# Closing normalisation with five of sixteen tiles divided otherwise over VectorE, ScalarE and GpSimd

## The reference

```python
def layer_norm(x, g, b):
    xf = x.astype(jnp.float32)
    mu = jnp.mean(xf, -1, keepdims=True)
    var = jnp.mean(jnp.square(xf - mu), -1, keepdims=True)
    y = (xf - mu) * lax.rsqrt(var + LN_EPS) * g.astype(jnp.float32) + b.astype(jnp.float32)
    return y.astype(x.dtype)
...
        ff = hierarchical_moe(x, w_group[l], b_group[l], w_router[l], b_router[l], w_gate_up[l], w_down[l])
        x = layer_norm(ALPHA * x + ff, ln2_g[l], ln2_b[l])
```

## Time and profile before

| | us |
|---|---|
| median of 3 runs | 2767.09 (2764.66 to 2777.89) |
| profiled execution, its own time | 2769.08 |
| its span, first to last instruction | 2767.4 |
| busy TensorE / VectorE / ScalarE / GpSimd over the span | 2570.9 / 1623.0 / 1206.0 / 497.0 |
| last matmul of the experts ends | 2702.4 |
| first load of the closing normalisation is issued | 2711.24 |
| last wide VectorE operation ends | 2763.2 |
| end of the span | 2767.4 |

### The profile page before, as it was taken

One profiled execution on the slowest core, in us unless ns is written; L12 is line 12 of the kernel. 1 busy time (PEld: TensorE's weight loads), 2 busy tenths in 40 slices (PEclk: granted clock), 3 DMA queues, 4 the chain that ended last, 5 costly groups with the idle time before them and its releaser, 6 DMA issues. The chain is left out here.

```text
span 2767.4 us, 42797 instructions
## 1 busy us (share of the span) xinstructions
PE 2570.9 (93%) x13455; PEld 2178.0 (79%) x13456; DVE 1623.0 (59%) x3059; ACT 1206.0 (44%) x2066; POOL 497.0 (18%) x538
## 2 busy tenths in 40 slices
PE   6999998999999999979799999769999999999990
PEld 4888886788888888879688888558888888888880
DVE  6333232766666666649644444569575567557956
ACT  4111111445445454437311010358575577557956
POOL 1111111101101010025323333112111122112210
PEclk9999999899999999979899999879999999999995
DMA  6444536756565564369534443459798778779956
GB/s 213 134 152 132 165 126 190 216 187 198 185 192 182 189 205 162 119 145 237 180 114 136 136 133 133 154 205 369 247 315 304 243 265 304 255 233 329 368 186 250
DMA packets 261763, 566.40 MB, mean 205 GB/s; under 512 B 27056, under 2 KB 119984, under 8 KB 259616
## 3 DMA queue, kind: packets, MB, share of 16 engines
q1 hardware_dynamic: 172816, 432.34, 45.9%
q0 software_dynamic: 18720, 64.96, 9.2%
q10 hardware_dynamic: 70128, 67.84, 7.3%
HBM read 433.45 MB, written 131.60 MB: 204 GB/s over the span
## 5 line engine op out<-in xcount | busy, mean ns | idle before, releaser
L2417 DVE TENSOR_TENSOR e_wl<-rw_raw,e_wh 128x1024 fp32r<-128x1024 f32 (+1 forms) x384 | 446.8, 1219 | 26.1 <-ACT e_wh L2330 25.8
L2330 ACT ACTIVATE e_wh<-rw_raw 128x1024 fp32r<-128x1024 f32 (+1 forms) x384 | 376.9, 1049 | 6.4 <-PEq L76 6.4
L1190 PE MATMUL b_pg<-b_g_wh,jb_w_low 128*128 128x512 f32 x1024 | 336.6, 401 | 0.7 <-DVE b_g_out L1385 0.7
L2280 PE MATMUL e_p_gu<-e_wh,e_xh 128*128 128x512 f32 (+1 forms) x784 | 310.5, 396 | 1.5 <-DVE e_xl L2422 1.5
L2282 PE MATMUL e_p_gu<-e_wl,e_xh 128*128 128x512 f32 (+1 forms) x784 | 306.2, 391 | 0.0
L2281 PE MATMUL e_p_gu<-e_wh,e_xl 128*128 128x512 f32 (+1 forms) x784 | 305.6, 390 | 0.0
L1190 PEld LDWEIGHTS b_pg<-b_g_wh,jb_w_low 128*128 128x128 f32 x1024 | 184.7, 189 | 33.4 <-issue 1.1
L1247 ACT ACTIVATE b_th<-b_t 128x512 fp32r<-128x512 f32 (+3 forms) x160 | 85.4, 534 | 284.5 <-PE b_t L1172 275.7
L1190 PE MATMUL b_pg<-b_g_wl,jb_w_low 128*128 128x512 f32 x512 | 204.4, 399 | 0.0
L1329 DVE TENSOR_SCALAR_CACHE_REDUCE b_sc<-b_s 128x512 f32<-128x512 f32 (+3 forms) x320 | 179.4, 606 | 31.9 <-PE b_s L1159 18.6
L300 PE MATMUL j_pg<-qkv_w_hi,j_xh 128*128 128x512 f32 (+1 forms) x512 | 190.9, 373 | 6.7 <-DVE qkv_w_lo L475 6.7
(11 more groups left out here) (363 smaller groups left out, 5866.3 us busy)
## 6 DMA issues: line engine op xcount, KB each, us to landing
rw_raw<-w_gate_up SPq DMA_DIRECT2D x256, 512.0 KB, 7.8
rw_raw<-w_down SPq DMA_DIRECT2D x128, 512.0 KB, 9.4
jb_w_low<-xt_hi SPq DMA_DIRECT2D x64, 512.0 KB, 3.8
jb_w_low<-xt_lo SPq DMA_DIRECT2D x64, 512.0 KB, 4.9
gates<-b_g_out ACTq DMA_DIRECT2D x64, 256.0 KB, 5.2
m_gt<-gates SPq DMA_DIRECT2D x16, 1024.0 KB, 8.2
qk_hi<-j_staged ACTq DMA_DIRECT2D x15, 832.0 KB, 4.5
qk_lo<-j_staged ACTq DMA_DIRECT2D x15, 832.0 KB, 6.9
```

The lines of the kernel that those rows point to most:

```text
L1190: last = nc.tensor.matmul(pg[:], x_side, w_side, start=(q == 0), stop=(q == PASSES - 1))
L2280: nc.tensor.matmul(p_gu[p][:], xh[:, at], hi, start=(k == 0), stop=False)
L2330: nc.scalar.activation(wh[:, slot(e, s), :], raw[:, s:s + 1, :], ACT.Copy).then_inc(w_hi, 1)
L2417: nc.vector.tensor_tensor(wl[:, slot(e, s), :], raw[:, s:s + 1, :], f(wh[:, slot(e, s), :]), ALU.subtract).then_inc(w_lo, 1)
```

## The change

Five tiles, TURNS = 2, 4, 7, 9, 12, take another way; the eleven others (MAIN) keep theirs, and their waits count positions in MAIN. For a turned tile VectorE takes bn_stats of both halves and bn_aggr (`statistics`), ScalarE a root of the variance (`root_of_turn`), VectorE a reciprocal and a one-column product, minus mean times reciprocal (`ready`), ScalarE one pass row * rs + shiftby in place (`centre`), and GpSimd the multiplication by gamma and the addition of beta, both in place. `statistics(0)` stands behind average(0), the others behind shift of every second main tile but the last; `ready` stands between scale and shift. The tile's store waits for GpSimd (`polished`). The order of loads and stores on SP stays.

```diff
--- before.py
+++ after.py
@@ -2138,6 +2138,14 @@
         z, gam, bet, junk = raw[:, 0:ROWS, :], raw[:, ROWS, :], raw[:, ROWS + 1, :], py[:]
         total, off, square, sd, rs = (ph.sb(n, [P, NT]) for n in ("total", "off", "square", "sd", "rs"))
         eps = ph.sb("eps", [P, 1])
+
+        TURNS = (2, 4, 7, 9, 12)
+        MAIN = [t for t in range(NT) if t not in TURNS]
+        bn = ph.sb("bn", [P, len(TURNS), 2, 6])
+        mv = ph.sb("mv", [P, len(TURNS), 2])
+        shiftby = ph.sb("shiftby", [P, len(TURNS)])
+        bn_step, bn_done, bn_root, bn_inv, bn_ready, centred, bn_times, polished, bn_passed = (ph.sem(n) for n in (
+            "bn_step", "bn_done", "bn_root", "bn_inv", "bn_ready", "centred", "bn_times", "polished", "bn_passed"))
         complete, vec_in, eps_set, loaded = ph.sem("complete"), ph.sem("vec_in"), ph.sem("eps_set"), ph.sems("loaded", ROWS)
         summed, averaged, squared, sd_done, inverted, times, finished, warmed = (
             ph.sem(n) for n in ("summed", "averaged", "squared", "sd_done", "inverted", "times", "finished", "warmed"))
@@ -2178,7 +2186,10 @@
                 sp.dma_start(row(t), acc[t * P:(t + 1) * P, :]).then_inc(loaded[t % ROWS], 16)
 
             def store(t):
-                sp.wait_ge(finished, t + 1)
+                if t in TURNS:
+                    sp.wait_ge(polished, TURNS.index(t) + 1)
+                else:
+                    sp.wait_ge(finished, MAIN.index(t) + 1)
                 sp.dma_start(out[0, t * P:(t + 1) * P, :], row(t)).then_inc(out_stored[t % ROWS], 16)
 
             wait_low(sp, NE - 1, NS - 1)
@@ -2242,6 +2253,12 @@
 
             pool.wait_ge(added, 16 * (b1 + 1))
             pool.sem_inc(complete, 1)
+            pool.wait_ge(vec_in, 32)
+            for n, t in enumerate(TURNS):
+                pool.wait_ge(centred, n + 1)
+                nc.gpsimd.tensor_tensor(row(t), row(t), gam, ALU.mult).then_inc(bn_times, 1)
+                pool.wait_ge(bn_times, n + 1)
+                nc.gpsimd.tensor_tensor(row(t), row(t), bet, ALU.add).then_inc(polished, 1)
             pool.wait_ge(gathered, 16 * (b1 + 1))
             settled(pool, passed)
 
@@ -2385,28 +2402,43 @@
 
             def add_up(t):
                 act.wait_ge(loaded[t % ROWS], 16 * (t // ROWS + 1))
-                if t:
-                    act.wait_ge(squared, t)
+                n = MAIN.index(t)
+                if n:
+                    act.wait_ge(squared, n)
                 nc.scalar.activation(junk, row(t), ACT.Identity, accum_out=total[:, t:t + 1]).then_inc(summed, 1)
 
             def spread(t):
-                act.wait_ge(averaged, t + 1)
+                act.wait_ge(averaged, MAIN.index(t) + 1)
                 nc.scalar.activation(junk, row(t), ACT.Square, bias=off[:, t:t + 1],
                                      accum_out=square[:, t:t + 1]).then_inc(squared, 1)
 
             def root(t):
-                act.wait_ge(squared, t + 1)
+                act.wait_ge(squared, MAIN.index(t) + 1)
                 nc.scalar.activation(sd[:, t:t + 1], square[:, t:t + 1], ACT.Sqrt, bias=eps[:], scale=1.0 / D).then_inc(sd_done, 1)
+
+            def root_of_turn(n):
+                t = TURNS[n]
+                act.wait_ge(bn_done, n + 1)
+                nc.scalar.activation(sd[:, t:t + 1], mv[:, n, 1:2], ACT.Sqrt, bias=eps[:]).then_inc(bn_root, 1)
+
+            def centre(n):
+                t = TURNS[n]
+                act.wait_ge(bn_ready, n + 1)
+                nc.scalar.activation(row(t), row(t), ACT.Identity, bias=shiftby[:, n:n + 1], scale=rs[:, t:t + 1]).then_inc(centred, 1)
 
             act.wait_ge(eps_set, 1)
             nc.scalar.activation(sd[:, 0:1], eps[:], ACT.Sqrt).then_inc(warmed, 1)
             act.wait_ge(warmed, 1)
             add_up(0)
-            for t in range(NT):
+            for n, t in enumerate(MAIN):
                 spread(t)
-                if t + 1 < NT:
-                    add_up(t + 1)
+                if n + 1 < len(MAIN):
+                    add_up(MAIN[n + 1])
                 root(t)
+                if n % 2 == 0 and n // 2 < len(TURNS):
+                    root_of_turn(n // 2)
+                if n % 2 and n // 2 < len(TURNS):
+                    centre(n // 2)
 
         @block.vector
         def _(dve):
@@ -2465,28 +2497,50 @@
             expert(NE - 1, True)
 
             def average(t):
-                dve.wait_ge(summed, t + 1)
+                dve.wait_ge(summed, MAIN.index(t) + 1)
                 nc.vector.tensor_scalar(off[:, t:t + 1], total[:, t:t + 1], -1.0 / D, None, ALU.mult).then_inc(averaged, 1)
 
             def scale(t):
-                dve.wait_ge(sd_done, t + 1)
+                dve.wait_ge(sd_done, MAIN.index(t) + 1)
                 nc.vector.reciprocal(rs[:, t:t + 1], sd[:, t:t + 1]).then_inc(inverted, 1)
                 if t == 0:
                     dve.wait_ge(vec_in, 32)
                 nc.vector.scalar_tensor_tensor(row(t), row(t), off[:, t:t + 1], gam, ALU.add, ALU.mult).then_inc(times, 1)
 
             def shift(t):
-                dve.wait_ge(inverted, t + 1)
-                dve.wait_ge(times, t + 1)
+                dve.wait_ge(inverted, MAIN.index(t) + 1)
+                dve.wait_ge(times, MAIN.index(t) + 1)
                 nc.vector.scalar_tensor_tensor(row(t), row(t), rs[:, t:t + 1], bet, ALU.mult, ALU.add).then_inc(finished, 1)
+
+            def statistics(n):
+                t = TURNS[n]
+                dve.wait_ge(loaded[t % ROWS], 16 * (t // ROWS + 1))
+                nc.vector.bn_stats(bn[:, n, 0, :], row(t)[:, 0:BANK])
+                nc.vector.bn_stats(bn[:, n, 1, :], row(t)[:, BANK:]).then_inc(bn_step, 1)
+                dve.wait_ge(bn_step, n + 1)
+                settled(dve, bn_passed)
+                nc.vector.bn_aggr(mv[:, n, :], bn[:, n, :, :]).then_inc(bn_done, 1)
+
+            def ready(n):
+                t = TURNS[n]
+                dve.wait_ge(bn_root, n + 1)
+                nc.vector.reciprocal(rs[:, t:t + 1], sd[:, t:t + 1]).then_inc(bn_inv, 1)
+                dve.wait_ge(bn_inv, n + 1)
+                dve.wait_ge(bn_done, n + 1)
+                nc.vector.scalar_tensor_tensor(shiftby[:, n:n + 1], mv[:, n, 0:1], -1.0, rs[:, t:t + 1], ALU.mult, ALU.mult).then_inc(bn_ready, 1)
 
             nc.vector.memset(eps[:], EPS / (ALPHA * ALPHA)).then_inc(eps_set, 1)
             average(0)
-            for t in range(NT):
-                if t + 1 < NT:
-                    average(t + 1)
+            statistics(0)
+            for n, t in enumerate(MAIN):
+                if n + 1 < len(MAIN):
+                    average(MAIN[n + 1])
                 scale(t)
+                if n % 2 == 0 and n // 2 < len(TURNS):
+                    ready(n // 2)
                 shift(t)
+                if n % 2 and n // 2 + 1 < len(TURNS):
+                    statistics(n // 2 + 1)
 
 
 def program(nc, a, out, phases=99):
```

## The result

The changed kernel takes 2774.46 us in the median (22 runs, 2767.94 to 2787.35), the one before 2769.31 beside it (22 runs, 2762.58 to 2778.6). The medians lie 5.2 us apart. The ratio over all the runs is 1.0023, interval 1.0013 to 1.0033: 6.4 us slower, between 3.6 and 9.1; the forecast was 9.7 more. The median lies in the forecast range (2773 to 2781) and within 0.5% of no change. The profiled execution of after took 2776.66 us, its span is 2774.9.

What follows compares the result with a forecast made beforehand. VectorE and ScalarE together bound the stage, transfers only its ends. Turns of 9.87 us for 8.3 and four queued last stores put the span's end at 2777.1 against 2767.4, +9.7: median 2776.8 us, range 2773 to 2781.

Steps and rivals of the forecast that it cites:

- The hold: Closing normalisation: VectorE operations with two SBUF inputs take turns with GpSimd's; 2.3 us lost on shift, 0.5 on scale.
- a four-column operation held 1.7 us: Window attention phase: two-input VectorE operation, 0.15 us alone, took 1.85 when begun inside a GpSimd operation.
- a chain of three that gave up 1.16: Earlier profile rows: three VectorE operations beside a GpSimd one took 4.82 us instead of 3.66.
- the walk: Step-by-step timing of VectorE, ScalarE and GpSimd through the closing normalisation, giving 9.87 us a turn.
- Rival 1: Closing normalisation: the engines do not disturb one another; span ends at 2766.6, time 2766 us; 8 in 100.
- rival 3: Closing normalisation: only part of an operation is held, half the loss, about +4, 2771 us; 7 in 100.
- The order in a turn: GpSimd's multiplication is asked for during the turn's second scale, with 0.7 us in hand against its coming ahead.
- rival 2: Centring precedes the turn's second scale: turn 11.8 us, total 2784.5; 18 in 100 together with held statistics.
- The size of a turn: Two common tiles and a turned one: 9.87 us, VectorE's own 7.54 plus 2.3, where three tiles took 8.3.
- The end: Last tiles: VectorE ends at 2771.45, four stores queue behind GpSimd's addition at 2768.95, last landing 2775.5, span end 2777.1.
- The total: Whole kernel: span 9.7 us longer, median 2776.8 us, starting from a median before of 2767.09.
- This costs nothing: Loads queued behind stores that wait for GpSimd are used over ten microseconds later, so their delay costs nothing.

Runs made afterwards that it cites:

- the fourth experiment: The changed kernel with stores, and the loads behind them, issued in the order in which tiles are finished; stage 62.4 us against 64.3.
- the PSUM version: The changed kernel with gamma and beta copied into idle PSUM tiles, read from there by VectorE; stage 57.1 us, ratio to the kernel before 0.9998.

## Why the prediction was right

**The hold.** Right, in kind and nearly in size. It was read from a four-column operation held 1.7 us and a chain of three that gave up 1.16, and it is there for 1024 columns: the long shift ends at 2736.47, 1.08 us behind the multiplication (2735.39), a little less than the 1.15 that the walk took for an operation that had waited. Rival 1 falls by the experiment without GpSimd (49.4 for 64.3), rival 3 because no wide operation with two SBUF inputs ended before the one that held it. The Trainium skill ("SBUF — State Buffer", section "Who interferes with whom") states that a VectorE instruction with two SBUF inputs contends with a GpSimd instruction that reads SBUF, and that one with at most one SBUF input, outside the two-port modes, does not. These traces agree: two SBUF inputs are held (3.18 us for 1.28), one in SBUF with one in PSUM is not (1275 ns), and bn_stats, with its single input, is not (0.68 us).

**The order in a turn.** Right. GpSimd asked at 2732.76, 0.84 us behind the start of the second scale at 2731.92; the walk had 0.7. That margin was worth naming: in the run in which the centring comes ahead of that scale the turn costs 11.2, where rival 2 had 11.8.

**The size of a turn.** Measured 9.37 where the walk had 9.87. VectorE's own work is 7.2 us without GpSimd's, not 7.54, and the two holds are 1.90 (shift, 3.18 for 1.28) and 0.45 (scale, 1.72 for 1.27); the walk labels them 2.3 and 0.5, which is 0.5 more than the 2.3 that its own turn has over 7.54. In the walk's own steps two terms were too dear. ready() cost 0.45 in the walk; from the end of the held scale (2739.76) to the start of shift (2739.96) it is 0.2, since its two small operations overlap their neighbours. And an operation that had waited ran shorter after the hand-over than the 0.1 us taken off: counted from the end of scale at 2733.18, the addition ends at 5.50 for 5.65, the held scale at 6.58 for 6.8. The centring took 1.23, not 1.1, which was hidden.

**The end.** The forecast ended VectorE 60.2 us into the stage (2771.45 less 2711.24), it ended at 58.6: four turns by 0.5 are 2.0 less, the second scale ended 0.6 later than in the walk (13.2 us into the stage for 12.6, tile 2 having come 0.9 later), and the last turn took 0.2 less. From the issue of store 12 to the last landing the sum has 6.5 us, the profile 6.5 (2766.8 to 2773.3). The order of the stores matters little: 1.4 us behind VectorE's end, by the fourth experiment.

**The total.** The stage was forecast 9.7 longer and is 8.1 longer in the profile, and the timed difference is 6.4 with an interval up to 9.1. The 1.6 us are the terms above. The rest lies within the scatter ahead of the stage and is left open; no run separates it. The total came closer (2776.8 for 2774.46) than the difference did, and that is in part luck: the forecast started from a median of three runs, 2767.09, and the 22 runs of the kernel before gave 2769.31.

**The loads.** "This costs nothing" was right for after, where ScalarE waits for no load but the first. It was right with less cover than the text said. Not all loads had ten microseconds: tile 13, issued at 2740.39, landed 6.5 us later and was read at 2748.96, 8.6 us behind its issue and 2.1 behind its landing. In the PSUM version the load of tile 13, late by the same queue, stood 2.45 us in the way.

## What to carry to other kernels

Before a part of an elementwise chain goes to GpSimd, list what VectorE does in the same stretch: every operation of it with two inputs in SBUF takes turns with GpSimd's, and part of the busy time given to GpSimd comes back as VectorE's (here 2.2 us a turn for GpSimd's 4.7; how much depends on what stands beside it). Put the operand in an idle PSUM tile, or lay one-input work (statistics, reductions) beside GpSimd. And where a queue works in tile order, a tile that is finished by a slower engine holds the loads and stores of all tiles behind it, which shows only when the rest has become quick.

## What the runs showed of the hardware

A one-column product with both inputs in SBUF is held like a wide one. In the PSUM version ready()'s product still reads two SBUF columns; GpSimd's addition ends at 2738.34 and the product, begun at 2738.03, lasts 0.33 us and ends at 2738.36, where in after the same product takes 0.16. It is the same in four of its five turns (0.30 to 0.41 us). GpSimd first, then VectorE:

```profile
2735.99 2.35 POOL L2264 TENSOR_TENSOR rw_raw<-rw_raw 128x1024 f32<-128x1024 f32 x1
...
2738.03 0.33 DVE L2533 SCALAR_TENSOR_TENSOR e_shiftby<-e_mv,e_rs 128x1 f32<-128x1 f32 x1
```

In this kernel the hold did not favour the engine with more queued: in every turn of after the one that waited first went first, though VectorE's operations stand back to back.
